# Gathered rows two blocks ahead, block 0 normalized at once, and scaled layer input as the start of the accumulators

## What is computed

```python
def peer_ffn(x, w_q, sub_keys, u, v):
    ...
        experts = i1 * PEER_N_KEYS + i2
        gates = jax.nn.softmax(cand_s, axis=-1)
        ue = jnp.take(u, experts, axis=0)
        ve = jnp.take(v, experts, axis=0)
        act = jax.nn.gelu(jnp.einsum('chkd,cd->chk', ue, xc), approximate=False)
        return jnp.einsum('chk,chkd->cd', gates.astype(xc.dtype) * act, ve)
...
        ffn = peer_ffn(x, peer_w_q[l], peer_sub_keys[l], peer_u[l], peer_v[l])
        x = layer_norm(DEEPNORM_ALPHA * x + ffn, ln2_g[l], ln2_b[l])
```

## Time and profile before

| | |
|---|---|
| median of three runs | 3308.46 us (3307.1 to 3309.74) |
| the profiled execution | 3310.66 us, span 3308.8 us |
| TensorE busy | 3209.9 us (97%) |
| TensorE weight loads | 2948.2 us (89%), beside the matmuls |
| VectorE busy | 2544.9 us (77%) |
| ScalarE busy | 1298.3 us (39%) |
| GpSimd busy | 1955.6 us (59%) |
| mean granted TensorE clock | 0.991 of full |

### The profile page before, as it was taken

How to read it: one execution, slowest core, us unless ns; L and a number is a source line. 1 busy time by engine, 2 the same in 40 slices (tenths; PEclk the granted TensorE clock), 3 DMA queues, 4 the chain that set the end, 5 groups by cost and what they waited for, 6 DMA issues and landing times. The chain is left out here.

```text
span 3308.8 us, 64646 instructions
## 1 busy us (share of the span) xinstructions
PE 3209.9 (97%) x18502; PEld 2948.2 (89%) x18502; DVE 2544.9 (77%) x5455; ACT 1298.3 (39%) x2054; POOL 1955.6 (59%) x1556
## 2 busy tenths in 40 slices
PE   8999999999999999999899999999999999999997
PEld 8898889999999888888798988899999998888886
DVE  1466567888888899999924655588888888999998
ACT  2355234444444333333324542344444443333332
POOL 3445338888654466666544443488886544666665
PEclk9999999999999999999999999999999999999999
DMA  4002139999787799999820011399997877999996
GB/s 168 28 1 77 39 90 303 321 321 307 249 299 249 262 337 335 338 338 332 280 96 25 1 77 51 101 315 320 321 314 247 292 253 265 339 339 336 337 331 216
DMA packets 249399, 765.14 MB, mean 231 GB/s; under 512 B 28384, under 2 KB 95712, under 8 KB 241376
## 3 DMA queue, kind: packets, MB, share of 16 engines
q1 hardware_dynamic: 170400, 459.95, 41.9%
q0 software_dynamic: 73728, 268.47, 21.6%
q10 hardware_dynamic: 5184, 35.65, 3.0%
HBM read 677.98 MB, written 85.98 MB: 231 GB/s over the span
## 5 line engine op out<-in xcount | busy, mean ns | idle before, releaser
L685 POOL TENSOR_TENSOR st_lo<-st_raw,st_hi 128x1024 fp32r<-128x1024 f32 x290 | 697.7, 2406 | 463.4 <-ACT st_hi L947 458.4
L947 ACT CAST st_hi<-st_raw 128x1024 fp32r<-128x1024 f32 x544 | 569.7, 1047 | 659.7 <-PE ps L1975 659.7
L1892 PE MATMUL ps<-t_hi,st_hi 128*128 128x384 f32 (+1 forms) x2288 | 794.6, 347 | 1.4 <-ACT st_hi L947 1.3
L1893 PE MATMUL ps<-t_lo,st_hi 128*128 128x384 f32 (+1 forms) x2288 | 786.8, 344 | 0.0
L793 POOL TENSOR_TENSOR wt_lo<-w_f,wt_hi 128x384 fp32r<-128x384 f32 x256 | 416.7, 1628 | 318.6 <-ACT wt_hi L1073 318.5
L1896 PE MATMUL ps<-t_hi,st_lo 128*128 128x384 f32 (+1 forms) x2288 | 462.3, 344 | 0.3
L1892 PEld LDWEIGHTS ps<-t_hi,st_hi 128*128 128x128 f32 x2288 | 430.2, 188 | 12.2 <-ACT st_hi L947 2.3
L1893 PEld LDWEIGHTS ps<-t_lo,st_hi 128*128 128x128 f32 x2288 | 430.1, 188 | 10.2
L1896 PEld LDWEIGHTS ps<-t_hi,st_lo 128*128 128x128 f32 x2288 | 408.3, 188 | 11.7 <-POOL st_lo L685 1.1
L990 ACT ACTIVATE h_out<-ps 128x384 f32<-128x384 f32 x256 | 125.7, 491 | 697.3 <-PE ps L1896 601.5
L1975 PE MATMUL ps<-st_hi,wt_hi 128*128 128x512 f32 x1536 | 390.0, 389 | 1.4 <-ACT wt_hi L1073 1.4
(11 more groups left out here) (218 smaller groups left out, 5097.7 us busy)
## 6 DMA issues: line engine op xcount, KB each, us to landing
st_raw<-in_peer_u SPq DMA_DIRECT2D x256, 512.0 KB, 4.2
st_raw<-in_peer_v SPq DMA_DIRECT2D x256, 512.0 KB, 4.8
gelu_d<-h_out SPq DMA_DIRECT2D x256, 192.0 KB, 5.3
h_in<-gelu_d SPq DMA_DIRECT2D x256, 192.0 KB, 5.5
gates_d<-g_stage ACTq DMA_DIRECT2D x32, 1024.0 KB, 6.0
g_ch<-gates_d SPq DMA_DIRECT2D x56, 512.0 KB, 6.2
w_raw<-in_w_in SPq DMA_DIRECT2D x16, 1168.0 KB, 5.2
st_raw<-in_peer_w_q SPq DMA_DIRECT2D x32, 512.0 KB, 3.6
```

The costliest lines, as they stand in the source:

```text
L685: nc.gpsimd.tensor_tensor(st_lo[:, s].rearrange("p c f -> p (c f)"), st_raw[:, r], st_hi[:, s].rearrange("p c f -> p (c f)").bitcast(F32), ...
L947: nc.scalar.copy(st_hi[:, r % 2].rearrange("p c f -> p (c f)"), st_raw[:, r]).then_inc(st_h, 1)
L1892: nc.tensor.matmul(dst, st_hi[:, s, c], t_hi[:, c, rows], start=c == 0, stop=False)
L1893: nc.tensor.matmul(dst, st_hi[:, s, c], t_lo[:, c, rows], start=False, stop=False)
```

## The change

Four edits:
1. The value stage's first four row adds stay, then two more follow (rows 4 and 5), and from then on two(b) adds row b+2; the two single adds at the end fall away. GpSimd's order follows: of the shares only share(0) comes before the fetches of rows 0 to 3, and afterwards share(n) stands ahead of the fetch of row n+3 in place of n+1.
2. VectorE starts acc with ALPHA times x_tok of block 0 in place of zeros. TensorE zeroes banks 4, 5 and 6 ahead of body 8 (open_sums), and ScalarE writes ALPHA times x_tok into one of them at the end of each of the bodies 8, 9 and 10; banks 2, 3 and 7 are zeroed where all six were. Banks 4 to 6 are block 2 and the first half of block 3.
3. total_stats adds the scaled input only to block 1 (whole) and to the second half of block 3.
4. Block 0 is normalized before the statistics of block 1; ScalarE's order follows, and in the last layer the statistics of block 2 come before shift.

```diff
             for b in range(VRING):
                 gather_v(0, 0, b, first=True)
-                if b < 2:
-                    share(b, b)
-            share(2, 0)
+                if b == 0:
+                    share(0, 0)
...
                     for k in range(VRING):
-                        share(8 * i + 4 * part + k + 3, 1 - k % 2)
+                        share(8 * i + 4 * part + k + 1, 1 - k % 2)
                         gather_v(g, 1 - part, k)
...
                         stage_body(w, w % 2, q, w < WIN - 1, 1)
+                        n = w * BODIES + q - B_ROUNDS
+                        bank = FREE_BANKS[n]
+                        act.wait_ge(acc_open, l + 1)
+                        nc.scalar.activation(ps[:, bank], x_tok[:, bank // 2, bank % 2 * T:(bank % 2 + 1) * T], ACT.Copy,
+                                             scale=ALPHA).then_inc(acc_set, 1)
...
-            nc.vector.memset(acc, 0.0).then_inc(w_ready, 1)
+            nc.vector.tensor_scalar(acc, x_tok[:, 0], ALPHA, None, ALU.mult).then_inc(w_ready, 1)
...
-            def two(b, r, slot, ahead=2):
+            def two(b, r, slot, ahead=2, lead=2):
...
-                    add_row(b + k, r + k)
+                    add_row(b + k + lead, (r + k + lead) % VRING)
...
+            two(0, 0, 0, lead=0)
+            two(2, 2, 2, lead=0)
+            for b in range(VRING, VRING + 2):
+                add_row(b, b % VRING)
...
             two(EB - 4, 0, 2 * GCH - 4, 1)
-            for b in range(EB - 2, EB):
-                add_row(b, b % VRING)
...
+                late = {RING_TB: 0, TB - 1: T}.get(tb)
+                if late is not None:
+                    rest = total[:, late:D]
+                    nc.vector.scalar_tensor_tensor(out=rest, in0=x_tok[:, tb, late:D], scalar=ALPHA, in1=rest,
+                                                   op0=ALU.mult, op1=ALU.add).then_inc(ffn_done, 1)
...
             total_stats(0)
+            normalize_total(0)
             total_stats(1)
-            normalize_total(0)
+            next_rest(0)
+            if l + 1 == L:
+                total_stats(2)
             shift(2 * l + 1)
...
+            pe.wait_ge(dots_kept, KEPT * (l + 1))
+            open_sums(FREE_BANKS).then_inc(acc_open, 1)
             with pe.Fori(B_ROUNDS, WIN * BODIES - 1) as body:
...
+            open_sums((2, 3, IOTA_BANK))
+            pe.wait_ge(acc_set, len(FREE_BANKS) * (l + 1))
```

More of the change, by code:

```diff
@@ L105 @@
 RAW = 4
+RING_TB = 1
+FREE_BANKS, IOTA_BANK = (4, 5, 6), 7
 LN_D = TB - 1
@@ L361, in build @@
     v_rows, ffn_done = sem("v_rows"), sem("ffn_done")
+    acc_open, acc_set = sem("acc_open"), sem("acc_set")
     waited = sem("waited")
@@ L811, in _ @@
             for k in range(VRING):
-                share(EB - 5 + k, 1 - k % 2)
+                share(EB - 7 + k, 1 - k % 2)
                 gather_v(EB // 4 - 1, 1, k)
-            share(EB - 1, 1)
+            for b in range(EB - 3, EB):
+                share(b, b % 2)
             if l + 1 < L:
@@ L1085, in _ @@
             tail = LN_TAIL[1]
-            for tb in range(tail + 1):
-                deviation(2 * l + 1, tb)
+            deviation(2 * l + 1, 0)
             if l + 1 < L:
                 round_first(l + 1)
+                round_tokens(3 * l + 3, 0)
+            deviation(2 * l + 1, 1)
+            if l + 1 == L:
+                deviation(2 * l + 1, 2)
             shifted(2 * l + 1, total_of(tail))
-            if l + 1 < L:
-                round_tokens(3 * l + 3, 0)
-            for tb in range(tail + 1, TB):
+            for tb in range(tail + 1 + (l + 1 == L), TB):
                 deviation(2 * l + 1, tb)
@@ L1951, in _, with open_sums @@
                         experts(2 * body + PRE + 1 + g // 4, g // 2 % 2)
+            def open_sums(banks):
+                for bank in banks:
+                    last = nc.tensor.matmul(ps[:, bank], zeros_bf[:, 0:P], zeros_bf[:, 0:T], start=True, stop=True,
+                                            skip_group_check=True)
+                return last
+            pe.wait_ge(dots_kept, KEPT * (l + 1))
+            open_sums(FREE_BANKS).then_inc(acc_open, 1)
             with pe.Fori(B_ROUNDS, WIN * BODIES - 1) as body:
@@ L1961, in _ @@
             pe.wait_ge(g_ev, TN // GRP * (l + 1) + RING)
-            for bank in range(2, 2 * TB):
-                nc.tensor.matmul(ps[:, bank], zeros_bf[:, 0:P], zeros_bf[:, 0:T], start=True, stop=True,
-                                 skip_group_check=True)
+            open_sums((2, 3, IOTA_BANK))
+            pe.wait_ge(acc_set, len(FREE_BANKS) * (l + 1))
             def gather(i, s, final=False):
```

22 lines of the change are left out of this document (14 added, 8 removed).

## The result

| | before | after |
|---|---|---|
| median | 3308.33 us (3305.79 to 3310.75, 19 runs) | 3314.31 us (3311.91 to 3318.42, 19 runs) |
| profiled execution | 3310.66 us, span 3308.8 | 3314.75 us, span 3312.9 |
| TensorE busy | 3209.9 us | 3213.5 us |
| VectorE busy | 2544.9 us | 2533.5 us |

What follows compares the result with a forecast made beforehand. TensorE bounds the value stage, with VectorE nearly as full, and VectorE's norm chain the time behind it. Gate bodies 3.1 + first blocks 8.7 - last layer's end 5.3 - first layer's end 2.1 = +4.4: 3312.9 us, range 3303.5 to 3318.5.

Steps and rivals of the forecast that it cites:

- Gate bodies, +3.1: Last gate bodies, both layers: zero matmuls ahead of body 8 +0.4, bank writes at two boundaries +0.59 each, per layer.
- The third write: ScalarE's bank write after body 10: free, since VectorE's one-hots set the pace there.
- First blocks, +8.7: First value blocks: TensorE waits for wt_lo in a loop through gate product, add and fetch, 4.4 and 4.3 us.
- The turns: Three rounds of wt_lo, gate product, add, fetch: 4.3 us, or 5.1 and 4.95 where st_lo stands in them.
- The first lateness: Start of the first layer's value stage: wt_lo(2) comes 2.4 us later than TensorE needs it.
- They put st_lo(6) about 1.9 us behind its trigger; ... covered: Value stage: the two extra adds delay st_lo(6), but TensorE wants it 2.9 behind; if uncovered, 1 us a layer.
- End of the last layer, -5.3: VectorE's norm chain: two adds and the residuals of block 0, block 2 and half of block 3 fall away.
- End of the first layer, -2.1: Next projection: turn of block 1 starts 2.1 sooner, behind GpSimd's w_lo and norm tail; ln_shift falls into second w_lo.
- Three zero matmuls less at the stage's start save nothing: Start of the value stage: no gain from fewer zero matmuls, since TensorE waits for wt_hi there.
- (A): Rival: the loop turns at 4.3, but VectorE and GpSimd do not hinder each other; 3306.3 us, chance 0.17.
- (C): Rival: the loop runs at its slow rows, 5.7 a turn; +9.9, 3318.4 us, chance 0.22.
- (B): Rival: TensorE never waits at the value stage's start and the bank writes hide; 3301 us, faster, chance 0.12.

Runs made afterwards that it cites:

- e2: Changed kernel without ScalarE's three bank writes, banks 2 to 7 all zeroed together before the value stage: 3312.03 us, ratio 1.0013.
- f5: Changed kernel with the three zero matmuls ahead of the value stage (banks 2, 3 and 7) issued twice: 3313.68 us, ratio 1.0017.
- e1: Changed kernel with GpSimd computing each share of wt_lo one fetch sooner, the two extra row adds kept: 3309.23 us, ratio 1.0004.
- g1: Changed kernel, GpSimd's order kept, with the two-row lead of adds built up at the start as in f6: 3307.77 us, ratio 0.9999.
- f6: Kernel of e1 with the two extra row adds removed and the first adds placed where VectorE waits for data: 3305.55 us, ratio 0.9993.
- e3: Changed kernel with ln_shift computed as tensor_scalar with one SBUF tensor operand in place of two: 3313.33 us, ratio 1.0018.
- f7: Kernel of f6 with e3's ln_shift, f5's doubled zeros, bank writes at body 10's end and behind the gelu of dots: 3300.4 us, ratio 0.9979.

## Why the prediction was right, and where not

The forecast, 3312.9 and +4.4, held; 3314.3 and +6.0 were measured, inside the range. Its mechanism held too: the closed loop through wt_lo, gate product, add and fetch is what costs. The size came out partly by luck, since errors in its parts cancel. By its own terms:

- **Gate bodies, +3.1.** The two waits grew by 0.51 each and the zero matmuls ahead of body 8 cost 0.20 (that body takes 8.56 in place of 8.36 us): 1.24 a layer, 2.5. The means over the kernels say about the same: the start of the stage lies at 1120.9 in the seven with writes at the ends of bodies 8 and 9 and 1119.8 in the six without, and "between" is 1107.2 against 1105.6, together 2.7. The third write was free, as predicted, and so was the scaling of block 0. The write took 0.60, as priced, but 0.1 of it was hidden.
- **First blocks, +8.7.** Measured 4.57 in the first layer, and 4.5 in the second in e2 and f5, where nothing else disturbs it: +9.1. e1 and g1 show that it is the loop. The turns were foreseen at 5.1, 4.95 and 4.3 and came at 4.93, 4.92 and 5.07; what made them up was partly something else, and their sum is near by luck. The meeting of wt_lo with st_lo costs 0.26 a turn and not 0.86, but the fetch starts 0.8 behind the end of the add for which it waits, where I had put 0.1 (before, that fetch stood behind a share, so no row showed it); and the third turn has GpSimd's copy of new indices in it. So most of what the turns last beyond 4.3 is the start of the fetch, about 0.7 a turn, and not the meeting of the two engines. The first lateness was 1.7 and not 2.4. The errors cancel.
- **"They put st_lo(6) about 1.9 us behind its trigger; ... covered"** held in the changed kernel: st_hi(6) ends at 1147.36, st_lo(6) runs from 1149.17, 1.8 behind it, to 1150.71, and TensorE starts the pass that needs it at 1152.53. Had it not waited for wt_lo(5), that would have been 1151.5, 0.8 later than st_lo(6) still. But the cover is the loop's work, which holds TensorE back as much as VectorE. Where e1 let TensorE go on, st_hi(6) ended at 1142.87 and st_lo(6) started at 1146.96, 4.1 behind, and the extra adds cost 1.34 and 1.43 us of waiting. The sum needed no term for this; what it cost is the e1 expectation, which took the whole loss of the loop for a gain.
- **End of the last layer, -5.3:** measured -5.48.
- **End of the first layer, -2.1:** -2.34 in the profile, -2.0 to -2.2 in e1, e2, f5, f6 and g1. ln_shift fell into the second w_lo as foreseen and ended as it did.
- **"Three zero matmuls less at the stage's start save nothing"** failed: they don't save, they cost. TensorE is left with 0.81 us of work between rests of 0.77 and 1.37, where it had 1.46 between 0.77 and 0.72, and in 8 of 14 cases the first block then runs for a while at the lower clock, for 1.6 us. Two layers at 8 in 14 make +1.8 on average. The prediction weighed the clock only behind the stage.

With these, 2.5 + 9.1 + 1.8 - 5.5 - 2.2 = +5.7, against 6.0 measured. The agreement is better than its parts deserve: f5, which should lie 1.8 below the changed kernel, is as far above before (5.9, with 3 us of uncertainty) as that one, and that a slow start costs the median what it costs a profile was argued and not shown.

Of the rivals, (A) asked for turns of 4.3 and (C) for 5.7: neither came. (A)'s premise, that the engines don't meet, is refuted by e3; but in the loop their meeting was worth only 0.26 a turn, so that (A) failed mostly by the late start of the fetch. (B), no wait at the start, is what f6 and g1 are, by other means; with the waits gone and the bodies and the clock mended (f7) the change is worth 7 us, as (B)'s 3301 had it.

## What to carry to other kernels

When an operation is moved in one engine's in-order program, write down the full cycle of waits through all engines, and compare its turn with the bottleneck's period; a cycle that is slower costs in every turn, and it can be cut wherever one member can start early. A lead over a steady loop is best built up where the engine waits anyway (here for the activations of block 4), and not by two operations more at a place with 0.3 us to spare. Removing idle-time work from ahead of a stretch of matmuls is not free by itself: look at the granted clock behind it, over several profiles.
